# Setup transposes in groups between matmuls, and gate chunk units moved inside the blocks of a trunk layer's first stage

## The reference

```
mod = silu(c) @ W_ada + b_ada -> shift1, scale1, gate1, shift2, scale2, gate2
h = RMSNorm(x) * (1 + scale1) + shift1
p = h @ W_in -> conv value | conv gate | ssm input u | ssm gate   (1024 columns each)
conv group: GLU -> causal depthwise conv(31) -> LayerNorm -> swish
ssm group:  64 groups of 16 channels, 64 complex states each, scan over positions,
            Re(C s) + D u -> gelu -> gate
x = x + gate1 * (concat of both, RMS-normed) @ W_out
h = RMSNorm(x) * (1 + scale2) + shift2
x = x + gate2 * MoE(h)     (4 groups of 8 experts, best group, best two experts, SwiGLU 512 wide)
out = RMSNorm(x)
```

## Time and profile before

| | |
|---|---|
| median of 3 runs | 1472.71 us (1469.9 to 1472.87) |
| the profiled execution's own time | 1473.02 us |
| its span, first to last instruction | 1471.1 us |
| mean granted TensorE clock | 0.978 of full |
| TensorE busy | 1345.1 us, 91% |
| VectorE busy | 538.8 us, 37% |
| ScalarE busy | 166.3 us, 11% |
| moved by DMA | 565.42 MB, 384 GB/s over the span |

### The profile page before, as it was taken

The page is one execution under the profiler, slowest core; times in us unless marked ns, Lnnn a source line. Parts: engine busy times, 40 slices in busy tenths (PEclk is TensorE's granted clock), DMA queues, the critical chain, the costliest instruction groups (busy, mean ns, idle before and its releaser), DMA issues.

```text
span 1471.1 us, 19330 instructions
## 1 busy us (share of the span) xinstructions
PE 1345.1 (91%) x8088; PEld 614.4 (42%) x8088; DVE 538.8 (37%) x953; ACT 166.3 (11%) x276; POOL 108.7 (7%) x112
## 2 busy tenths in 40 slices
PE   5999999999999989999899899899799899889986
PEld 2766777666544443333333333333233333333321
DVE  4241999999968530111121021021021112112104
ACT  3041100003212240000000000010010000000001
POOL 1000007401100035000000000000000000000000
PEclk9799999999999999999999999999999999999999
DMA  9999866999759789999999999999999999999994
GB/s 345 346 386 397 305 213 250 362 401 381 290 195 364 316 368 413 431 426 428 428 428 428 429 429 429 428 429 429 428 428 428 429 429 429 429 429 429 427 425 194
DMA packets 84942, 565.42 MB, mean 384 GB/s; under 512 B 7736, under 2 KB 7920, under 8 KB 49760
## 3 DMA queue, kind: packets, MB, share of 16 engines
q1 hardware_dynamic: 82848, 561.35, 93.5%
q10 hardware_dynamic: 2048, 3.43, 0.6%
HBM read 562.62 MB, written 2.13 MB: 384 GB/s over the span
## 4 chain that ended last, share of the span: by engine, by line
PE 53%; DMA 23%; PEld 9%; issue 6%; DVE 6%; SPq 2%; PEldq 1%; ACT 1%; DVEq 0%; ACTq 0%
PE ps L1245 16%; PE ps L1208 16%; DMA ring<-in_exp_w_down 10%; PEld ps L845 7%; DMA ring<-in_exp_w_gate 6%; DMA ring<-in_exp_w_up 5%; PE ps L990 4%; PE ps L1163 4%; PE ps L1257 3%; PE ps L845 2%; PE ps L744 2%; DVE arena L1937 2%; PE ps L689 2%; PE ps L705 1%; PE ps L1006 1%
## 5 line engine op out<-in xcount | busy, mean ns | idle before, releaser
L1208 PE MATMUL ps<-ring,arena 128*64 128x512 f32 x1984 | 459.9, 605 | 48.1 <-DMA ring<-in_exp_w_up 34.1
L1208 PEld LDWEIGHTS ps<-ring,arena 128*64 128x64 f32 x1984 | 152.7, 139 | 327.7 <-issue 326.8
L1245 PE MATMUL ps<-ring,arena 128*32 128x512 f32 x2048 | 247.2, 608 | 26.4 <-DMA ring<-in_exp_w_down 19.3
L845 PE MATMUL ps<-arena,ring 128*128 128x256 f32 x896 | 201.6, 382 | 0.3 <-issue 0.3
L845 PEld LDWEIGHTS ps<-arena,ring 128*128 128x128 f32 x896 | 168.0, 190 | 41.3 <-issue 19.6
L1245 PEld LDWEIGHTS ps<-ring,arena 128*32 128x32 f32 x2048 | 58.5, 110 | 177.7 <-issue 176.0
L2223 DVE TENSOR_TENSOR arena<-arena,ps 128x512 f32<-128x512 f32 x64 | 41.0, 684 | 206.5 <-PE ps L1257 206.4
L2198 DVE TENSOR_SCALAR arena<-ps,mod 128x256 f32<-128x256 f32 x56 | 30.4, 544 | 195.0 <-PE ps L1163 195.0
L2212 DVE TENSOR_TENSOR arena<-arena,ps 128x512 f32<-128x512 f32 x16 | 11.0, 687 | 234.1 <-PEq L1214 231.7
L1975 DVE SCALAR_TENSOR_TENSOR arena<-arena 128x256 f32<-128x256 f32 x240 | 96.0, 477 | 0.0
L990 PE MATMUL ps<-ring,arena 128*128 128x512 f32 x192 | 83.8, 594 | 1.3 <-ACT arena L1462 1.3
(11 more groups left out here) (278 smaller groups left out, 819.6 us busy)
## 6 DMA issues: line engine op xcount, KB each, us to landing
ring<-in_exp_w_down SPq DMA_DIRECT2D x60, 2048.0 KB, 17.1
ring<-in_exp_w_gate SPq DMA_DIRECT2D x59, 2048.0 KB, 15.2
ring<-in_exp_w_up SPq DMA_DIRECT2D x59, 2048.0 KB, 16.3
ring<-in_w_ada SPq DMA_DIRECT2D x96, 1024.0 KB, 10.8
ring<-in_w_in SPq DMA_DIRECT2D x32, 1024.0 KB, 11.2
ring<-in_w_out SPq DMA_DIRECT2D x16, 1024.0 KB, 7.8
ring<-in_exp_w_gate SPq DMA_DIRECT2D x8, 1024.0 KB, 8.0
ring<-in_exp_w_down SPq DMA_DIRECT2D x8, 1024.0 KB, 17.3
```

Source lines behind the costliest of these rows:

```text
L845: last = mm(ps[:, j // 2, (j % 2) * T:(j % 2 + 1) * T], ring[:, s, kk * N + j * P:kk * N + (j + 1) * P], hT[:, k, :], start=(k == 0 and j ...
L1208: last = mm(ps[64 * x:64 * x + 64, stage, :], xT[:, k, slot:slot + SLOTS], unit[:, kk * N:(kk + 1) * N], start=(k == 0), stop=(k == KD - 1 ...
L1245: last = mm(ps[dst:dst + 32, 2 + n, :], hidT[pr][:, u, src:src + 32], job_unit(m, x, False)[:, n * N:(n + 1) * N], start=(u == 0), stop=(u ...
```

## The change

The order of units in stage A is new: a block's chunk unit no longer follows its u unit directly, but (for blocks 1 and 2) stands between the scale units and the shift units of the next block. The groups of transposes are cut smaller and put between the quarters of a chunk unit or between `W_ada` units. ScalarE's and VectorE's orders follow. The kernel does the same instructions as before; on SyncE's queue the same 39 units come in the new order.

```diff
-for _b in range(FIRST_STEP):
-    A_LIST += [("u", _b, 0), ("in", _b, 0)]
-    A_LIST += [("scale", _b + 1, i) for i in range(4)] + [("shift", _b + 1, i) for i in range(4)]
-A_LIST += [("u", 3, 0)]
+A_LIST += [("u", 0, 0), ("in", 0, 0)]
+for _b in range(1, 4):
+    A_LIST += [("scale", _b, i) for i in range(4)]
+    if _b > 1:
+        A_LIST += [("in", _b - 1, 0)]
+    A_LIST += [("shift", _b, i) for i in range(4)] + [("u", _b, 0)]
...
+            def first_chunk(n, between):
+                chunk_unit(n, 0, A_LIST[n][1], between)     # between(kk) runs ahead of quarter kk
+
+            def block_2(kk):
+                if kk == 1:
+                    columns(4)
+                if kk == 2:
+                    turn_blocks(1)
+                if kk == 3:
+                    turn_blocks(2)
+
+            def block_3(kk):
+                if kk == 1:
+                    columns(6)
+                if kk == 2:
+                    turn_blocks(4)
+                if kk == 3:
+                    turn_blocks(5)
...
-            a_units(8, 9)
-            turn_b()
+            a_units(8)
+            first_chunk(9, turn_b)
             a_units(10, 11, 12, 13)
-            turn_router(0)
             columns(2)
-            turn_router(1)
-            a_units(14, 15, 16, 17)
+            for i in range(4):
+                a_units(14 + i)
+                turn_router(i)
+            turn_router(4)
+            columns(3)
+            a_units(18, 19, 20, 21, 22)
             turn_blocks(0)
-            turn_blocks(1)
-            columns(3)
-            a_units(18, 19, 20, 21, 22, 23)
-            turn_blocks(2)
+            first_chunk(23, block_2)
+            a_units(24, 25, 26, 27)
             turn_blocks(3)
-            columns(4)
-            a_units(24, 25, 26, 27)
-            turn_blocks(4)
-            turn_blocks(5)
             columns(5)
-            a_units(28, 29, 30, 31, 32, 33)
+            a_units(28, 29, 30, 31, 32)
+            first_chunk(33, block_3)
+            a_units(34, 35, 36, 37)
             turn_blocks(6)
             turn_blocks(7)
-            columns(6)
-            a_units(34, 35, 36, 37)
             columns(7)
             a_units(38)
```

`turn_b` takes a quarter (8 transposes) and runs before each quarter of the first chunk unit; `turn_router` takes a part (8 transposes for parts 0 to 3, the last four for part 4). On ScalarE the order is now:

```diff
-            column_copy(2)
-            column_copy(3)
-            keep_drive(0)
-            keep_drive(1)
+            for x in range(2, 5):
+                column_copy(x)
+            for r in range(3):
+                keep_drive(r)
             act.wait_ge(phase_ready, 1)
             ...                                  # sine of the tables, twice
-            column_copy(4)
-            keep_drive(2)
+            column_copy(5)
             keep_drive(3)
             ...                                  # absolute value, twice
-            column_copy(5)
+            column_copy(6)
             keep_read(4)
             keep_read(5)
             ...                                  # cosine, twice
-            column_copy(6)
             keep_read(6)
             keep_read(7)
             ...                                  # copy of the router weights (line 1429), two DMAs
             column_copy(7)
```

More of the change, by code:

```diff
@@ L772, in turn_small, with turn_b @@
                 last.then_inc(cw_turned, 1)
[L775 to L783, removed]
+            def turn_b(quarter):
+                if quarter == 0:
+                    pe.wait_ge(b_landed, 16 * 2)
+                    pe.wait_ge(cw_stored, 1)
+                c = quarter // 2
+                for h in range(quarter % 2 * 8, quarter % 2 * 8 + 8):
+                    last = tr(ps[:, 4 + c, h * 32:(h + 1) * 32],
+                              bst[:, c, :].rearrange("p (s h) -> p h s", h=HG)[:, h, :], 32)
+                if quarter == 3:
+                    last.then_inc(b_turned, 1)
             def turn_router(part):
-                pe.wait_ge(bdiag_ready, 1)
                 if part == 0:
+                    pe.wait_ge(bdiag_ready, 1)
                     pe.wait_ge(wr_landed, 16 * 5)
-                    for e in range(EXP):
+                if part < NG:
+                    for e in range(part * NE, (part + 1) * NE):
                         o = P * (NG + e // NE * NE) + e % NE
@@ L796, in turn_router @@
                         last = tr(ps[:, 5, e * KD:(e + 1) * KD], wst[:, e:e + (P - 1) * NG + 1:NG], KD)
-                last.then_inc(wr_turned, 1)
+                if part >= NG - 1:
+                    last.then_inc(wr_turned, 1)
             def turn_blocks(r):
@@ L832, in ada_unit, with chunk_unit @@
                     pe.drain().then_inc(ada_done, 1)
-            def chunk_unit(n, it, u, middle):
+            def chunk_unit(n, it, u, between):
                 s = arrived(n)
                 for kk in range(4):
-                    if kk == 2:
-                        middle()
+                    between(kk)
                     k = 4 * u + kk
@@ L962, in _ @@
                     side(3 * g)
-                    chunk_unit(n, i, k, lambda: side(3 * g + 1))
+                    chunk_unit(n, i, k, lambda kk: kk == 2 and side(3 * g + 1))
                     side(3 * g + 2)
@@ L1883, in _ @@
                         link(ins)
+            columns(2)
             dve.wait_ge(wr_turned, 1)
             V.tensor_copy(wr_early[:, :, NG:], ps[:, 4, :].rearrange("p (e k) -> p k e", e=EXP)).then_inc(wr_staged, 1)
-            columns(2)
             dve.wait_ge(wr_turned, 2)
```

2 lines of the change are left out of this document (removed).

## The result

The changed kernel takes 1475.31 us (median of 13 runs, 1469.4 to 1479.96) against 1469.90 for the kernel before, run beside it (13 runs, 1465.24 to 1473.75): ratio 1.0036, 95% interval 1.0025 to 1.0047, so 5.4 us slower. The changed kernel's profiled execution took 1479.96 us, its slowest, and stands 6.9 us above the profiled one of before (1473.02).

The account below looks back on a forecast made before the run. TensorE was taken to bound stage A, its last u unit setting the end: 3.3 us gained, 3.0 given back through ScalarE, 0.9 + 0.8 lost to the clock, 1.4 later, so 1474.5 us; range 1469.5 to the slower rival, own range 1471.5 to 1476.

Parts of the forecast that it names:

- One for one to the end: Whatever moves the end of stage A's last u unit, 141.36, moves the kernel's end by as much.
- Chunk and `turn_b` together end at 59.73 as before: In stage A, block 0's chunk unit and `turn_b`, interleaved in quarters, take no longer together than before.
- Scale1 at full clock: Behind the quartered `turn_b`, block 1's scale units take 3.64 us instead of 6.33.
- Shift1 "at full clock 3.64", with the router transposes between its units: Block 1's shift units take 3.64 us, with 3.67 + 0.66 us of router transposes between them.
- the slower rival: Alternating router transposes and shift1 units lets the clock fall: 2.7 + 1.7 us more, +5.8 in all, 1478.5; chance 0.33.
- Block 1's u unit, 1.7 us lost: After 3.1 us without dense work this unit loses 1.7 us to the clock, within bounds 0 and 2.7.
- Block 2's u unit, a coin's throw taken as no loss: This unit starts at 103.3 and loses nothing to the clock, within bounds 0 and 1.7.
- The loads' cap at unit 33: Block 2's chunk unit can't start before its weights land at 113.0; forecast to come at 113.9, without waiting.
- the forecast of no wait: Ahead of `turn_b`, the later B matrix lands at 45.5, before it is needed at 49.06.
- ScalarE's order, 3.0 us of which columns(7) waits some 2.5: Behind shift3, ScalarE's copies delay `columns(7)`; the last u unit starts 5.66 behind instead of 2.67, giving back 3.0 us.
- The last u unit at 9.71: After 4.5 us with little TensorE work, this unit takes 9.71 us, 0.9 more than before.
- the 0.8 us for `columns(7)` at the lower clock: Ahead of the last u unit, `columns(7)` runs at half clock, 1.87 us for 1.05, adding 0.8.

Follow-up runs that it names:

- the chunk-move run: The changed kernel with `turn_b` and the router transposes each in one block as before, leaving the chunk units' move and ScalarE's new order: ratio 1.0040 to the kernel before.
- the second: A second profile of the unedited changed kernel, timed again for another draw: ratio 1.0037 to the kernel before.
- the first experiment: The changed kernel with `column_copy(7)` ahead of `keep_read(6)`, `keep_read(7)` and the router weights' copy on ScalarE: ratio 1.0015 to the kernel before.
- the split chunk unit: The kernel before with `turn_b` in quarters and block 2's chunk unit in two halves, the second behind shift3 around `columns(7)`: ratio 0.9980.
- the filler runs: The changed kernel with 12 unused transposes behind each of block 3's four scale units, of 16 or 128 rows: 1478.72 and 1483.6 us.

## Why the prediction was right, and where not

The forecast was no change that can be measured, 1.4 us later by the profile; what came is 5.4 us slower, the case that I gave a third. That 1474.5 lies near the measured 1475.31 is partly luck: it stood on a base of 1472.71, 2.8 us above the 1469.90 measured beside the changed kernel, and the loss was forecast 3.6 us too small. In the trace the last u unit ends at 148.59 (139.76 + 8.83) and not at 142.7. Of these 5.9 us 3.9 arose between scale1 and block 1's u unit, 1.2 and 1.8 in the u units of blocks 1 and 2 and 0.8 ahead of scale1; the last u unit gave 1.7 back.

- *One for one to the end*: right, 7.23 us at the scan, 7.0 at the end, and within 3.0 us over all traces.
- *"Chunk and `turn_b` together end at 59.73 as before"*: wrong by 1.0 us. Cut into quarters they take 11.67 us and not 10.67.
- *Scale1 at full clock*: right (3.64), and as forecast the router transposes no longer wait for VectorE, which was done at 64.5 where they start at 66.92. But of the 2.7 us the quarters take back 1.0. With the router's block right behind scale1 VectorE would have bound it anyway, by the 2.28 us of the chunk-move run.
- *Shift1 "at full clock 3.64", with the router transposes between its units*: the step that failed. I took the alternation at full clock, with no row that shows such a mix. The four units take 6.68 us (1.06 + 1.74 + 1.94 + 1.94) and `columns(3)` 1.87 instead of 0.95. This is the mechanism of the slower rival, that the alternation doesn't hold the clock; the rows show it in seven of the eight traces. The rival's price for it, 2.7, is near the 3.0 measured.
- *Block 1's u unit, 1.7 us lost*: the fall is there, the size was 2.8 in the first trace and 2.3 in the second (9.41).
- *Block 2's u unit, a coin's throw taken as no loss*: 1.7 lost in the first trace, none in the second. The rival counted it. In the nine traces with this order around it the unit was slow twice, so taking it at no loss was the better guess.
- *The loads' cap at unit 33*: not reached in the changed kernel, as the chunk unit came at 121.6 and not at 113.0. In the fast trace of the first experiment that unit came at 112.10, without a wait. Loads do bound the fast traces, but elsewhere: 0.3 to 0.7 us for weights in shift1, and 1.0 to 1.7 us ahead of `turn_b` for the second B matrix in three of them, where the forecast of no wait went by a slow u unit of block 0.
- *ScalarE's order, 3.0 us of which columns(7) waits some 2.5*: right to the tenth (2.97 and 2.50), and by the first experiment worth 3.1 us of the 5.4. What the other 2.3 are, the ratios don't divide safely: covering `columns(2)` gives back 1.5, putting the router back 1.2, where each ratio alone is known to about 1.7 us either way. By the traces some 2 us arise from the first chunk unit to the end of block 1's u unit.
- *The last u unit at 9.71*: 8.83 and 9.04 in the two traces; and the 0.8 us for `columns(7)` at the lower clock came in the second only (1.86, 1.05 in the first). I over-sized it.
- The trace that I worked from was one of the slow draws of before: 1473.02 us, with the median of the 13 runs at 1469.90. The clock losses that I counted as regained are not lost in every execution, so part of the gain side was never there on average. That is the likeliest reason why the median's change is larger than the sum of my terms; it is argued, not shown. What the record does show is that the traces of before had a low clock: 0.978 on average in both, where the runs of before beside the experiments, in three sets of 29, 23 and 28, have medians of 0.982, 0.980 and 0.981, and those with the higher clock are the faster ones (correlations of -0.64 to -0.87). An average doesn't tell which stretch was slow.

## What to carry to other kernels

When a late step is moved past a wait, walk the queue of every engine that serves it: here four small stores and a copy, harmless while the transposes that they wait for came early, held up the one copy that TensorE was waiting for, and ate 3 us. Before counting a regained clock as a gain, look at what is waited for next; a slow stretch that ends in a wait for another engine costs little. To keep the clock ahead of a critical unit, put large matmuls between its last dependencies, as the split chunk unit does; small transposes between the shift1 units did it in one of eight traces. And cutting two stretches of work into quarters has its own price, here 1.0 us.

## What the runs showed of the hardware

- The clock can stay at its lower level through a stretch in which TensorE is busy nearly all the time: 8.86 of 9.00 us busy at a granted clock of 0.51, with 16-row transposes and `W_ada` units in turn. It isn't the mixture alone: in the filler runs the clock stayed at 1.00, with 128-row transposes (9.76 of 9.90 us busy) and with 16-row ones from one source (7.36 of 7.50).
- The slower level stretches the `W_ada` units (1.06 to 1.94 us) but not the small transposes between them (1.05 and 1.06 us for eight).
- Matmuls in short groups take longer: 32 transposes of 32 rows and the 32 matmuls of a chunk unit took 10.6 to 10.7 us as two runs of 32, and 11.6 to 11.7 as eight groups of 8 in turn.
- Executions of one kernel spread over 8.5 us (before) and 10.6 us (changed); at least part of this is the clock in stage A, as the same u unit took 9.54 and 7.14 us in two traces of one kernel.
